# The norms between the stages of a two-block float32 transformer: sums without GpSimd, roots on columns, and first blocks step by step of the contraction

## What is computed

```python
def first_block(x, ...):
    x = x + 0.5 * rms_norm(swiglu(rms_norm(x, ffn1_pre_g), ffn1_w_gu, ffn1_w_down), ffn1_post_g)
    y = hybrid_mixer(rms_norm(x, mix_pre_g), w_in, ...)        # RG-LRU and window attention, then w_o
    x = x + rms_norm(y, mix_post_g)
    return x + 0.5 * rms_norm(swiglu(rms_norm(x, ffn2_pre_g), ffn2_w_gu, ffn2_w_down), ffn2_post_g)

def second_block(x, c, ctx, ...):                              # i = 0: retention, i = 1: neighbourhood attention
    a = modulate(h, m[0], m[1])                                # h * (1 + scale) + shift
    h = layer_norm(ALPHA * h + m[2] * mixer(a), ln_g[i, 0], ln_b[i, 0])
    f = swiglu_2(modulate(h, m[3], m[4]), ffn_w13[i], ffn_w2[i])
    h = layer_norm(ALPHA * h + m[5] * f, ln_g[i, 1], ln_b[i, 1])
```

## Time and profile before

| | |
|---|---|
| median of 3 runs | 3171.98 us (3170.32 to 3172.51) |
| the profiled execution | 3176.37 us, its span 3174.6 us |
| mean granted clock of TensorE | 0.969 of full speed |
| TensorE busy | 2997.0 us, 94% |
| VectorE busy | 1512.0 us, 48% |
| ScalarE busy | 1035.2 us, 33% |
| GpSimd busy | 802.2 us, 25% |
| HBM read | 262.54 MB, 83 GB/s over the span |

### The profile page before, as it was taken

One profiled execution on the slowest core, in us unless ns is written; L12 is line 12 of the kernel. 1 busy time (PEld: TensorE's weight loads), 2 busy tenths in 40 slices (PEclk: granted clock), 3 DMA queues, 4 the chain that ended last, 5 costly groups with the idle time before them and its releaser, 6 DMA issues. The chain is left out here.

```text
span 3174.6 us, 39520 instructions
## 1 busy us (share of the span) xinstructions
PE 2997.0 (94%) x15816; PEld 2511.5 (79%) x15816; DVE 1512.0 (48%) x2412; ACT 1035.2 (33%) x1758; POOL 802.2 (25%) x540
## 2 busy tenths in 40 slices
PE   7999996899998999999998899999969999999998
PEld 7888874788788768788785888888958687888887
DVE  5667576465675424232425545454371514532224
ACT  4322344443323322222223521121253424342223
POOL 3333332343333211011111311111152212232222
PEclk9999997999999999999999999999989999999999
DMA  4545221135452211111110133233212021123331
GB/s 154 164 151 169 84 88 34 33 113 160 143 162 94 87 34 61 46 54 54 40 60 7 47 127 102 79 116 103 70 51 93 22 73 31 48 81 99 93 100 60
DMA packets 84759, 268.77 MB, mean 85 GB/s; under 512 B 9056, under 2 KB 16608, under 8 KB 84192
## 3 DMA queue, kind: packets, MB, share of 16 engines
q1 hardware_dynamic: 84576, 266.25, 26.2%
HBM read 262.54 MB, written 2.10 MB: 83 GB/s over the span
## 5 line engine op out<-in xcount | busy, mean ns | idle before, releaser
L1008 PE MATMUL ps<-t_h,t_whi 128*128 128x512 f32 (+1 forms) x2736 | 978.4, 358 | 53.7 <-DVE t_wlo L1521 27.4
L1009 PE MATMUL ps<-t_h,t_wlo 128*128 128x512 f32 (+1 forms) x2736 | 968.6, 354 | 0.0
L1010 PE MATMUL ps<-t_h,t_whi 128*128 128x512 f32 (+1 forms) x2736 | 967.3, 354 | 0.0
L1932 POOL TENSOR_TENSOR t_wlo<-t_raw,t_whi 128x1024 fp32r<-128x1024 f32 (+3 forms) x203 | 483.8, 2383 | 1669.9 <-ACT t_whi L1241 1669.9
L1008 PEld LDWEIGHTS ps<-t_h,t_whi 128*128 128x128 f32 x2736 | 525.9, 192 | 131.6 <-issue 28.5
L1521 DVE TENSOR_TENSOR t_wlo<-t_raw,t_whi 128x1024 fp32r<-128x1024 f32 (+3 forms) x203 | 263.7, 1299 | 675.8 <-ACT t_whi L1241 675.7
L1009 PEld LDWEIGHTS ps<-t_h,t_wlo 128*128 128x128 f32 x2736 | 526.7, 193 | 69.5 <-issue 1.0
L1010 PEld LDWEIGHTS ps<-t_h,t_whi 128*128 128x128 f32 x2736 | 525.9, 192 | 69.1
L1008 PE MATMUL ps<-t_hid,t_whi 128*128 128x256 f32 (+1 forms) x1656 | 538.0, 325 | 11.0 <-DVE t_hid L1639 7.5
L1009 PE MATMUL ps<-t_hid,t_wlo 128*128 128x256 f32 (+1 forms) x1656 | 533.2, 322 | 0.0
L1010 PE MATMUL ps<-t_hid,t_whi 128*128 128x256 f32 (+1 forms) x1656 | 532.4, 322 | 0.0
(11 more groups left out here) (220 smaller groups left out, 2703.1 us busy)
## 6 DMA issues: line engine op xcount, KB each, us to landing
t_raw<-in_gu SPq DMA_DIRECT2D x176, 512.0 KB, 3.6
t_raw<-in_ada SPq DMA_DIRECT2D x96, 512.0 KB, 3.7
t_raw<-in_dn SPq DMA_DIRECT2D x48, 448.0 KB, 3.3
t_raw<-in_dn SPq DMA_DIRECT2D x24, 512.0 KB, 3.5
t_raw<-in_ret_v SPq DMA_DIRECT2D x16, 512.0 KB, 3.5
t_raw<-in_ret_qk SPq DMA_DIRECT2D x16, 512.0 KB, 3.5
t_raw<-in_ret_g SPq DMA_DIRECT2D x16, 512.0 KB, 3.5
t_raw<-in_ret_o SPq DMA_DIRECT2D x16, 512.0 KB, 3.7
```

The costliest lines, as they stand in the source:

```text
L1008: e.matmul(out, whi, xlo, start=first, stop=False)
L1009: e.matmul(out, wlo, xhi, start=False, stop=False)
L1010: return e.matmul(out, whi, xhi, start=False, stop=last)
L1932: e.tensor_tensor(m.WLO[:, j % NH, 0:n], m.RAW[:, it.raw % NR, 0:n], m.WHI[:, j % NH, 0:n], ALU.subtract).then_inc(*S["lo_pool"].of(j))
```

## The change

1. **Steps.** The first four blocks of the mixer and of each FFN are given to `together`: for each chunk `k` of the contraction all four blocks are multiplied, into two banks with two halves of 256 columns each, before the next chunk. The value rows of retention's first head and attention's first half go by steps too, two tiles at a time; attention's tiles are taken latent first.
2. **Sums.** GpSimd's adds (L1948) go to VectorE. The sum for a layer norm's mean starts as chunk 0 plus chunk 2, with no copies by ScalarE. The squares and sums of the norms before the mixer and both first-block FFNs leave the send chain for a chain of their own, beside the steps.
3. **Roots on columns.** `root_sum` makes the accumulators the stationary operand (four float32 matmuls of one column), so that the sum of a token stands in one of 2 columns of 128. ScalarE's root and VectorE's reciprocal are of 128x2. `root_diag` scales the identity by it, and `root_row` (two float32 matmuls of 128 columns against the constant) lays it back on all partitions, in PSUM bank 6 or 7, from where the multiplies read it.
4. **Who does what in the sends.** The add to x is VectorE's (`norm_add`). ScalarE makes the full and the high version of a modulated chunk; VectorE the low half. Multiplying x by ALPHA comes later, in a chain of its own. GpSimd keeps weights' low halves, gates and the work inside the stages.
5. **Order in microseconds.** `tick` is given the length of the products just put, and the chains' waits are in microseconds.
6. **Parts.** `PARTS2` is turned round, and the last part (four blocks wide) loads two `down` blocks in one slot: 402 weight loads in place of 406. The third FFN ends with the latent tokens first.

The diff, cut to what the prediction speaks of:

```diff
-PARTS2 = (4, 4, 4, 5, 5)
+PARTS2 = (5, 5, 4, 4, 4)
...
+SUB3 = ((0, 256), (256, 256), (512, 256))
...
-            chains[s][0] = wait
-
-    def tick():
+            chains[s][0] += wait
+
+    def tick(us):
+
         for s in sorted(chains):
-            chains[s][0] -= 1
-            if chains[s][0] <= 0:
+            chains[s][0] -= us
+            while s in chains and chains[s][0] <= 0:
                 step(s)
...
                         last = ("ps", g.id)
+                        tick(nk * (n + 32) / 800)
                         post(g)
-                        tick()
...
+    def together(specs, segs):
+
+
+
+        held = [block(sp[0], sp[1]) for sp in specs]
+        for si, (t0, n) in enumerate(segs):
+            force_tokens(t0, n)
+            groups, posts, two = [], [], []
+            for i, ((_, _, nk, src, outs), j) in enumerate(zip(specs, held)):
+                (_, emptier, post), = outs
+                if i < 2:
+                    two.append(bank())
+                    g = put("group", w=j, t0=t0, n=n, bank=two[i], po=0, before=seat(two[i], emptier, len(items)), ends=[])
+                else:
+                    g = put("group", w=j, t0=t0, n=n, bank=two[i - 2], po=256, before=[], ends=[groups[i - 2].id, len(items)])
+                    owner[g.bank].append((emptier, g.id))
+                groups.append(g)
+                posts.append(post)
+            for k in range(nk):
+                put("step", groups=groups, k=k, nk=nk, src=src, t0=t0, n=n)
+                tick(len(groups) * (n + 32) / 800)
+            for g, j, post in zip(groups, held, posts):
+                if si == len(segs) - 1:
+                    over(j, "ps", g.id)
+                post(g)
+        return ("ps", groups[-1].id)
...
+        size = 2 if pairs else 1
+        for i in range(0, 6, size):
...
+    def root(inst, s, eps, b, before):
+
+        i = turn["root"] = turn.get("root", 0) + 1
+        put("root_sum", inst=inst, s=s, eps=eps, bank=b, before=before, col=i % 4 * 2)
+        yield 1.8
+        off, after, keys = tmp("b", 256)
+        free(keys, ("ps", ("rs", inst, s)))
+        put("root_diag", inst=inst, s=s, off=off, after=after, col=i % 4 * 2)
+        yield 0.7
+        put("root_row", inst=inst, s=s, off=off, bank=b)
...
+    def before_norm(inst, s, after):
+
+        for c in range(DC):
+            sum_add(inst, s, c, "x", [], True)
+            yield 0.5
+        yield 0.5
+        b = chain_bank()
+        yield from root(inst, s, RMS_EPS, b, seat(b, "rs", (inst, s)))
+        yield 0.4
+        put("rs_copy", inst=inst, s=s, bank=b, after=after)
...
             if pi == 0:
-                columns(specs[:4], subs, batch=4)
+                together(specs[:4], subs)
                 specs = specs[4:]
...
+    def step(it):
+        k = it.k
+        xhi, xlo = moving(it, k)
+        for g in it.groups:
+            if k == 0:
+                w.wait_ge(lo_of(g.w), g.w)
+                wait_all(g.before)
+            slot = g.w % NH
+            done = products(m.ps(g), m.WHI[:, slot, k * P:(k + 1) * P], m.WLO[:, slot, k * P:(k + 1) * P], xhi, xlo,
+                            k == 0 and not g.po, k == it.nk - 1, True)
+            if k == it.nk - 1 and g.ends:
+                done.then_inc(*S["ps"].of(*g.ends))
...
+    def root_sum(it):
+
+        w.wait_ge("acc", (it.inst, it.s, 7))
+        wait_all(it.before)
+        for i in range(2):
+            for c in (6, 7):
+                done = e.matmul(m.PS[:, it.bank, i:i + 1], m.acc(it.s, c)[:, i * P:(i + 1) * P], m.one1024[:, 0:1],
+                                start=c == 6, stop=c == 7, skip_group_check=True)
+        done.then_inc(*S["ps"].of(("root", it.inst, it.s)))
+
+    def root_row(it):
+
+        w.wait_ge("root_dve", ("diag", it.inst, it.s))
+        for i in range(2):
+            done = e.matmul(m.root_row(it.bank)[:, i * P:(i + 1) * P], m.one1024, m.tmp(it.off + i * P, P), start=True, stop=True,
+                            skip_group_check=True)
+        done.then_inc(*S["ps"].of(("rs", it.inst, it.s)))
...
+    def root_diag(it):
+        r, scale = m.ST[:, it.col:it.col + 2], 1024.0
+        w.wait_ge("root_act", ("sqrt", it.inst, it.s))
+        e.reciprocal(r, r).then_inc(*S["root_dve"].of(("recip", it.inst, it.s)))
+        wait_all(it.after)
+        w.wait_ge("root_dve", ("recip", it.inst, it.s))
+        for i in range(2):
+            done = e.tensor_scalar(m.tmp(it.off + i * P, P), m.ident, r[:, i:i + 1], scale, ALU.mult, ALU.mult)
+        done.then_inc(*S["root_dve"].of(("diag", it.inst, it.s)))
...
-        e.scalar_tensor_tensor(out=f, in0=f, scalar=m.par(it.post, it.j), in1=m.rs(it.s * 256, 256), op0=ALU.mult, op1=ALU.mult).then_inc(
+        w.wait_ge("ps", ("rs", it.inst, it.s))
+        e.scalar_tensor_tensor(out=f, in0=f, scalar=m.par(it.post, it.j), in1=m.root_row(it.bank), op0=ALU.mult, op1=ALU.mult).then_inc(
             *S["f_scaled"].of((it.inst, it.j, it.s)))
```

410 lines of the change are left out of this document (204 added, 206 removed).

## The result

| | before | after |
|---|---|---|
| median of 7 runs each | 3173.99 us (3170.32 to 3175.64) | 3184.05 us (3177.34 to 3184.52) |
| span of the profiled execution | 3174.6 us | 3182.7 us |
| mean granted clock | 0.969 | 0.971 |

The account below looks back on a forecast made before the run. It took TensorE's idle time in six passages between stages as the bound. Gains of 63 us, less 4 for pre-norms and 1 at the start, made 58 off 3176.4, and 4.4 lower for the median: 3114 us, range 3070 to 3166.

Parts of the forecast that it names:

- six passages: Changes from one stage to the next, from first FFN to fourth FFN; of 128 us lost there, 68 would be left.
- rival (a): Waits for a fourth weight or slot eat the gains of steps at the passages: 28 us go, 3142; chance 0.22.
- (c): Rival: root_row as a new wait, 22 with some 20 us counted; at 4 us each, slower, 3182; chance 0.10.
- Two signs of being wrong: Of three listed: waits for a fourth weight's low half over 5 us each; single-column passes over 0.2 us.
- Part 1: Steps: waits for chunks 1 to 7 go; waits for four weights and some 1.4 us at five fifth blocks come.
- Part 4: The passages walked over the new engine orders: gains of 8, 8, 13, 12, 10 and 9 us, 3 at the end.
- The walk of the first passage: First FFN to mixer: fourth weight split at 392.7, 512-column products at 420.5 instead of 428.30, 8 us gained.
- The fifth block: In each stage done by steps: it waits some 1.4 us for a freed slot, at five places.
- Part 3: Roots on columns: a norm costs TensorE -0.24 to +0.64 us, upper end taken; root_row is a new wait.
- Part 2: Sums and norms without GpSimd: a variance sum 2.0 us instead of 2.5; each norm's path 0.85 us shorter on VectorE.
- Value rows in pairs: Second FFN to retention: value rows in pairs by steps remove both gaps and their low clock but about 3 us: 13.
- Pre-norms in chains of their own: Six pre-norms beside steps: their root passes on TensorE cost 6 x 0.64 = 4 us.

Follow-up runs that it names:

- e6: The changed kernel with a bank for each of a step's four groups, so each signals its own end: 3177.43 us, 1.0010 against the kernel before.
- e12: The changed kernel with root_row put into TensorE's queue 3.0 us of products after the diagonal instead of 0.7: 3179.57 us, 1.0011 against before.
- e3: The changed kernel with full-width roots again (one join of 256 columns, reciprocal on 128x256, no root_row): 3184.05 us, 1.0023 against before.
- e7: e6 with steps of two blocks at a time instead of four: 3179.75 us, 1.0017 against the kernel before.
- e8: The changed kernel with even chunks' sums and the adds to x back on GpSimd: 3176.45 us, 1.0011 against the kernel before.
- e10: e9 with the edit of e8 (even sums and adds to x on GpSimd): 3172.93 us, 0.9995 against the kernel before.
- e9: e6 with the edit of e4 (value rows one tile at a time): 3173.82 us, 0.9995 against the kernel before.
- e4: The changed kernel with retention's and attention's first value rows one tile at a time again: 3178.61 us, 1.0008 against the kernel before.
- e2: The changed kernel with block by block order in the first FFN's first four blocks alone: 3187.05 us, 1.0030 against the kernel before.
- e5: The kernel before with steps alone in the mixer and four FFNs, each group in its own bank: 3252.98 us, 1.0249 against before.
- e1: The changed kernel with the first four blocks of the mixer and four FFNs block by block again: 3197.38 us, 1.0067 against before.

## Why the prediction was wrong

**Where the sum failed.** Of the 60 us forecast for the six passages the profile after shows 12. The start loses 9.6 us for 1, the rows between the passages lose 9 for nothing, and the end 1.5 where 3 were to be gained. The step that failed is that of Parts 1, 2 and 4 that takes VectorE's chain at its instructions' own lengths: the fourth weight, the sums and the diagonal come later than walked, since they stand in VectorE's queue behind sends and weights' halves and are held by GpSimd. In kind this is rival (a) with a part of (c). Two signs of being wrong came true in part: a fourth weight cost 5.51 us for a limit of 5 at one place (2.79 at the second FFN), and the passes of one column take over 0.2 us at the lower clock (below).

**What held.** Which work bounds the kernel (idle time in the passages) stands. The sizes of single instructions held: `root_sum` takes the upper end, and so does `root_row`. Two of each from the start of the first FFN, with the products behind them:

```profile
28.34 1.84 PE L1170 MATMUL ps<-t_con,t_misc 128*128 128x1 f32 x16
30.04 0.36 PE L1080 MATMUL ps<-t_h,t_whi 128*128 128x256 f32 x1
...
32.99 1.05 PE L1178 MATMUL ps<-t_tmp,t_con 128*128 128x128 f32 x8
33.80 0.37 PE L1080 MATMUL ps<-t_h,t_whi 128*128 128x256 f32 x1
```

(30.04 - 28.34) / 2 = 0.85 us for eight passes of one column, 0.106 each, and (33.80 - 32.99) / 2 = 0.40. An estimate by the page TensorE: Matmul & The Clock Gate of the Trainium skill (LDWEIGHTS), 128 columns divided by 1.2, so 107 ns for a load, agrees with the 0.106. It does not hold at the lower clock. In the second FFN's passage, at a granted clock of 0.50, the eight passes take 676.90 - 675.17 = 1.73 us, 0.216 each:

```profile
675.17 1.86 PE L1170 MATMUL ps<-t_con,t_misc 128*128 128x1 f32 x8 [5.21 <-DVE t_misc L1650]
676.90 0.56 PE L1080 MATMUL ps<-t_h,t_whi 128*128 128x256 f32 x1
```

The same holds at 1055.15, behind 5.29 us. The upper end of the prediction doubles where a `root_sum` comes late. The passages from retention to third FFN and on to attention went the way I said, at -6.3 and -7.9 for -12 and -10.

**The fourth weight (Part 1, Part 4).** I wrote that it would be split at 392.7. It was split at 406.12. Of this, 10.9 us are the kernel's delay by the end of the last `down` product (384.0 before, 394.9 after). The walk has the split 8.7 us behind that end, and it came 11.2 behind: 2.5 us more, in VectorE's queue ahead of the last product's add. 1.9 of them are the add of x at 392.76 that GpSimd held. The release of the slot, at 394.9, isn't what the cast waited for. The walk of the first passage then misses by 8.3 us in sum (438.37, less the 9.6 of delay at the last `down` products, against 420.5). The norm's passes and a 0.63 us wait among the last `down` products take 1.35 (which with the 9.6 makes the 10.9). The fourth weight takes 2.5. From there to the end of the first half are 16.1 us for 13.0: after the gap 15 products run at 0.21 us in place of 0.12 (1.35), and waits of 0.91 and 0.15 lie in it: with what the norm's passes take beyond the walk, 3.1 in all. The second half is 0.5 longer, the fifth block's wait 0.8. That is 8.3: no single term, but a stop that is paid once more in clock. The same step failed at the start, where I had 1 us and where gaps of 3.02, 0.81 and 1.21 lie in the first twelve products, and in part at the second FFN (1.31 and 2.79, with 5.21 for a `root_sum` behind them). At the fourth FFN it is the chain alone: 4.98 for the first `root_row`, then 2.85 and 4.55 for chunks.

**The fifth block.** 2.16 us instead of 1.4, because I let each group free its slot when its own products end, and the code signals the halves of a bank together. e6 shows 1.44 with signals apart.

**`root_row` (rival (c)).** I put its waits at 20 us and the limit for a loss at 3.5 us for each of 22. They are 29.4 us in ten, with 19.9 for `root_sum`. The longest, 10.13, 7.99 and 4.98, stand where a stage's last products have ended and nothing else is in TensorE's queue. The mechanism of (c) is real, but it isn't the main cause: taken away in part by e12, it came back as waits for chunks, and e3, which has no `root_row` at all, is no faster. Nor was it a matter of the weights alone: in e7 their waits are nearly gone, and those for `root_row` are longer. What the passages wait for is the length of the chain on VectorE, whichever instruction at its end TensorE meets. Part 3 priced the diagonal at 0.9 us with hand-over; one of its two scalings was held for 2.28 to 2.37 us in three norms.

**Sums on one engine (Part 2).** I counted it as a gain of 0.5 us a sum and 0.85 a norm. e8 has the reverse sign, 3176.45 for 3184.05, with intervals that overlap a little, and e10 against e9 has none, so neither a gain nor a loss of this part is shown. The add's price was right when free, 0.42 us. The mean of the 48 adds to x, though, is 569 ns:

```profile
L1697 DVE TENSOR_TENSOR t_x<-t_x,t_misc 128x256 f32<-128x256 f32 x48 | 27.3, 569 | 0.0
```

The range had at most 12 us for this. But I took contention as the doubling of the earlier trace rows (0.94 for 0.47). With 2.4 us instructions of GpSimd beside it a VectorE instruction can take 2.27. What it costs is set by whether a weight's half happens to start just ahead. I also left the scaling L1659 out of it, which was held as well.

**Value rows in pairs.** Retention's were forecast at 13 us; 1.0 was measured, and 3.6 without them (e4). The gaps for weights in the earlier trace rows did go, but a `root_sum` of 5.29 us took their place. To a new wait of this kind I had given a price only at `root_row` (rival (c)).

**Pre-norms in chains of their own.** I charged their passes (4 us) and not the two waits each puts in TensorE's queue. With blocks at the start the loss stays without any steps (+10.6 in e2), but no run puts the old roots there as well, so that it is theirs alone isn't shown.

**Behind the mixer's first blocks.** I had nothing for it, and +4.8 was measured. Steps deliver the outputs of all four blocks at once, at the end, and the small work that the mixer does with them starts late; TensorE stands 3.11 us at 444.10. The stretch is at +3.3 to +5.0 in every changed kernel with steps of four blocks (+5.9 in e5), +1.7 with two (e7), and 0.0 with none (e1).

**Still open.** At the start no order that was tried gives less than +6 us. Of the 6.6 us between the medians of after and e6 the table's places give only 1.7 with certainty, behind the second FFN's first blocks. And which of the differences between the old and the new norm chains costs the 23.4 us of e1 stays open: neither the roots (e3) nor the engine of the adds (e10 against e9) is shown to.
